# Inverting 64x64 triangular blocks of a recurrence: the lower levels in 32x32 tiles of TensorE on half the columns

## The reference

```python
def step(state, inp):
    r_t, w_t, k_t, v_t, kk_t, a_t = inp
    sa = jnp.einsum('bhvk,bhk->bhv', state, -kk_t)
    state = (state * w_t[:, :, None, :]
             + sa[..., None] * (kk_t * a_t)[:, :, None, :]
             + v_t[..., None] * k_t[:, :, None, :])
    return state, jnp.einsum('bhvk,bhk->bhv', state, r_t)
state0 = jnp.zeros((B, H, N, N), jnp.float32)
_, o = lax.scan(step, state0, ...)
```

## Time and profile before

| | |
|---|---|
| Median of 3 runs | 2298.42 us (2294.25 to 2299.28) |
| The profiled execution | 2297.4 us, its span 2295.6 us |
| Instructions in the span | 35212 |
| PE busy | 2162.0 us, 94% |
| DVE, ACT, POOL busy | 1228.8, 860.6, 996.5 us |
| The long stage of `rwkv` | from 210.5 us; levels 1 to 5 from 230.07 to 282.87; chunk loop from 297.1 |

### The profile page before, as it was taken

How to read it: one execution, slowest core, us unless ns; L and a number is a source line. 1 busy time by engine, 2 the same in 40 slices (tenths; PEclk the granted TensorE clock), 3 DMA queues, 4 the chain that set the end, 5 groups by cost and what they waited for, 6 DMA issues and landing times. The chain is left out here.

```text
span 2295.6 us, 35212 instructions
## 1 busy us (share of the span) xinstructions
PE 2162.0 (94%) x13161; PEld 1743.4 (76%) x13161; DVE 1228.8 (54%) x1928; ACT 860.6 (37%) x1345; POOL 996.5 (43%) x524
## 2 busy tenths in 40 slices
PE   6997998799999999899889999999999889999998
PEld 4675985688888888777667888888777568888887
DVE  3367526877505772432664577731398564777601
ACT  3445224433313332332364433332232754333322
POOL 4224111344534444365552444444456644444442
PEclk8999999899999999999899999999999999999999
DMA  4220012133332333233102333333333003333232
GB/s 126 65 65 25 4 30 61 56 102 99 110 91 84 100 91 110 78 83 83 46 1 60 88 101 101 91 90 97 102 75 91 1 19 92 95 101 97 87 101 87
DMA packets 347085, 177.10 MB, mean 77 GB/s; under 512 B 20835, under 2 KB 344158, under 8 KB 346974
## 3 DMA queue, kind: packets, MB, share of 16 engines
q1 hardware_dynamic: 346476, 175.47, 26.8%
q10 hardware_dynamic: 210, 0.08, 0.0%
q0 software_dynamic: 288, 0.03, 0.0%
HBM read 173.44 MB, written 2.11 MB: 76 GB/s over the span
## 5 line engine op out<-in xcount | busy, mean ns | idle before, releaser
L312 POOL TENSOR_TENSOR wlo<-raw,whi 128x1024 fp32r<-128x1024 f32 (+3 forms) x347 | 793.2, 2288 | 1081.6 <-ACT whi L871 603.8
L325 PE MATMUL banks<-xhi,whi 128*128 128x512 f32 x1688 | 668.8, 396 | 6.7 <-DVE cb L1034 3.9
L326 PE MATMUL banks<-xlo,whi 128*128 128x512 f32 x1688 | 659.0, 390 | 0.0
L327 PE MATMUL banks<-xhi,wlo 128*128 128x512 f32 x1688 | 658.9, 390 | 0.0
L325 PEld LDWEIGHTS banks<-xhi,whi 128*128 128x128 f32 x1688 | 318.1, 188 | 82.8 <-issue 13.6
L326 PEld LDWEIGHTS banks<-xlo,whi 128*128 128x128 f32 x1688 | 318.1, 188 | 68.2 <-issue 3.6
L327 PEld LDWEIGHTS banks<-xhi,wlo 128*128 128x128 f32 x1688 | 318.0, 188 | 67.0
L961 ACT ACTIVATE cb<-banks,conv 128x512 f32<-128x512 f32 x152 | 118.0, 779 | 438.7 <-DVE banks L1023 438.7
L871 ACT ACTIVATE whi<-raw 128x1024 fp32r<-128x1024 f32 (+2 forms) x208 | 204.9, 989 | 186.1 <-DMA raw<-in_ffn_w_out_dram 78.9
L326 PE MATMUL banks<-glo,whi 128*128 128x512 f32 x608 | 236.5, 389 | 0.0
L325 PE MATMUL banks<-ghi,whi 128*128 128x512 f32 x608 | 236.5, 389 | 0.0
(11 more groups left out here) (450 smaller groups left out, 2615.8 us busy)
## 6 DMA issues: line engine op xcount, KB each, us to landing
raw<-in_ffn_w_in_dram SPq DMA_DIRECT2D x88, 512.0 KB, 3.8
raw<-in_w_ffn_up_dram SPq DMA_DIRECT2D x64, 512.0 KB, 4.1
raw<-in_w_ffn_down_dram SPq DMA_DIRECT2D x32, 512.0 KB, 3.7
raw<-in_ev_w_in_dram SPq DMA_DIRECT2D x25, 512.0 KB, 4.0
raw<-in_ffn_w_out_dram SPq DMA_DIRECT2D x32, 384.0 KB, 3.4
raw<-in_ffn_w_out_dram SPq DMA_DIRECT2D x32, 320.0 KB, 3.3
raw<-in_od_w_in_dram SPq DMA_DIRECT2D x20, 512.0 KB, 3.9
raw<-in_w_in_dram SPq DMA_DIRECT2D x16, 512.0 KB, 3.8
```

Of the source, the lines that this page charges most:

```text
L312: return pool.tensor_tensor(wlo[c][:, 0:n, :], raw[b][:, 0:n, :], whi[c][:, 0:n, :].bitcast(F32), ALU.subtract)
L325: pe.matmul(acc, whi[b][:, k, :], hi(k), start=first and k == 0, stop=False)
L326: pe.matmul(acc, whi[b][:, k, :], lo(k), start=False, stop=False)
L327: mm = pe.matmul(acc, wlo[b][:, k, :], hi(k), start=False, stop=last and k == n - 1)
```

## The change

The levels up to blocks of 32 work on the two diagonal 32x32 blocks of each 64x64 matrix alone. T, the transposed seed `sTt` and pm keep 256 columns a tile: 8 heads of 32, where partition group g of 32 (of four) holds block g % 2 of chunk g // 2. A group of these kinds is 32 matmuls of 32x32, on the four diagonal tiles of the array in turn (`SPREAD`), into four banks of 64 columns, and a take-out has 128x256 values. There are two such bank sets, so a group waits for the group two before it (`held`). The level from 32 to 64 becomes two kinds: `plast` (16 matmuls into the lower group's partitions, copied by ACT) and `ttlast`, whose first matmuls (`up`) give the off-diagonal block and whose second transpose the lower diagonal block of T. A new kind `s0` transposes T for the seed (ACT), in place of POOL's eight operations; POOL now places the upper diagonal blocks in Tt, one operation a tile after `tt` of level 4. The turns stand ahead of `p0`. `nt`, `ak`, `y`, `w`, `u` and the chunk loop are as before. The packed masks have 9 parts of 64 columns in place of 10.

```diff
+                order = [("nt", t, 0) for t in range(NT)] + [("turn", x, 0) for x in range(8)]
+                FINE = len(order)
+                order += [(kind, t, 0) for kind in ("p0", "s0") for t in range(NT)]
+                for l in range(1, LEVELS - 1):
+                    for kind in ("p", "tt", "t"):
                         order += [(kind, t, l) for t in range(NT)]
+                order += [(kind, t, 0) for kind in ("plast", "ttlast") for t in range(NT)]
+                WIDE = len(order)
                 order += [(kind, t, 0) for kind in ("ak", "y", "w", "u") for t in range(NT)]
...
+                def held(n):
+
+                    if n < FINE or n >= WIDE + 4:
+                        return [n - 4] if n >= 4 else []
+                    if n < WIDE:
+                        return [n - 2] if n >= FINE + 2 else [n + (n - FINE) - 4, n + (n - FINE) - 3]
+                    return [WIDE - 2 + (n - WIDE) // 2]
...
+                SPREAD = [(g, (i + g) % 4, i // 4) for i in range(8) for g in range(4)]
...
+                def quad(n):
+                    return banks[:, 4 * (n % 2):4 * (n % 2) + 4, 0:2 * SUB].rearrange("p h (q n) -> p q h n", q=2)
...
                     for t in range(NT):
-                        wait_taken(pool, where["nt", t, 0])
-                        pool.tensor_tensor(four(Tt[:, t, :]), four(nt[:, t, :]), mask(TURNED), ALU.mult).then_inc(seeded.h, 1)
-                        pool.wait_ge(seeded.h, 2 * t + 1)
-                        pool.tensor_tensor(four(Tt[:, t, :]), four(Tt[:, t, :]), mask(EYE), ALU.add).then_inc(seeded.h, 1)
+                        wait_taken(pool, where["tt", t, LEVELS - 2])
+                        pool.tensor_scalar(Tt[:, t, :].rearrange("p (a s n) -> p a s n", a=8, s=2)[:, :, 0, :],
+                                           sTt[:, t, :].rearrange("p (a n) -> p a n", a=8), masks[:, WHERE, 0:1], None, ALU.mult)                            .then_inc(placed.h, 1)
...
+                        elif kind == "w":
+                            pe.wait_ge(placed.h, t + 1)
...
+                        elif FINE <= n < WIDE:
+                            for g, hh, q in SPREAD:
+                                x = sub(g)
+                                to = g + (1 if kind == "plast" else 0)
+                                if kind == "plast" and g % 2 or kind == "ttlast" and not g % 2:
+                                    continue
+                                o = banks[sub(to), 4 * (n % 2) + hh, q * SUB:(q + 1) * SUB]
+                                if kind == "p0":
+                                    mm = pe.matmul(o, nt[x, t, column(q, hh, g % 2)], ident[x, x], start=True, stop=True)
+                                elif kind == "s0":
+                                    mm = pe.matmul(o, T[x, t, small(q, hh)], ident[x, x], start=True, stop=True)
+                                elif kind == "t":
+                                    mm = pe.matmul(o, sTt[x, t, small(q, hh)], ident[x, x], start=True, stop=True)
+                                elif kind == "ttlast":
+                                    up = banks[sub(g - 1), 4 * (n % 2) + hh, q * SUB:(q + 1) * SUB]
+                                    pe.matmul(up, pm[x, t, small(q, hh)], sTt[x, t, small(q, hh)], start=True, stop=True)
+                                    mm = pe.matmul(o, T[x, t, small(q, hh)], ident[x, x], start=True, stop=True)
+                                elif kind in ("p", "plast"):
+                                    mm = pe.matmul(o, nt[x, t, column(q, hh, to % 2)], T[x, t, small(q, hh)], start=True, stop=True)
+                                else:
+                                    mm = pe.matmul(o, pm[x, t, small(q, hh)], sTt[x, t, small(q, hh)], start=True, stop=True)
...
                         elif kind == "p0":
-                            chain(dve.tensor_tensor(four(T[:, t, :]), acc, mask(0), ALU.mult))
-                            ins = dve.tensor_tensor(four(T[:, t, :]), four(T[:, t, :]), mask(EYE), ALU.add)
+                            chain(dve.tensor_tensor(smalls(T[:, t, :]), quad(n), small_mask(0), ALU.mult))
+                            ins = dve.tensor_tensor(smalls(T[:, t, :]), smalls(T[:, t, :]), small_mask(EYE), ALU.add)
...
+                        elif kind == "ttlast":
+                            ins = dve.tensor_copy(Tt[:, t, :].rearrange("p (q h s n) -> p q h s n", q=2, h=4, s=2)[:, :, :, 1, :], quad(n))
```

More of the change, by code:

```diff
@@ L32 @@
 EHALF = math.exp(-0.5)
-TURNED, BEFORE, UPTO, EYE = LEVELS, LEVELS + 1, LEVELS + 2, LEVELS + 3
+SUB = C // 2
+EYE, WHERE, BEFORE, UPTO = LEVELS - 1, LEVELS, LEVELS + 1, LEVELS + 2
 CST = {}
 _at = 0
-for _name, _w in (("ident", P), ("ones", P), ("pair", P), ("swap", P), ("packed", 10 * C), ("future", P), ("future_own", P),
+for _name, _w in (("ident", P), ("ones", P), ("pair", P), ("swap", P), ("packed", 9 * C), ("future", P), ("future_own", P),
                   ("inside", S), ("freq", 2), ("onehot", RLEN), ("flip", P)):
@@ L75, in constants @@
     ri, ci = row % C, col[:, 0:C]
-    levels = [(ri >> l + 1 == ci >> l + 1) & (ri >> l & 1 == 1) & (ci >> l & 1 == 0) for l in range(LEVELS)]
-    turned = (ri >> 1 == ci >> 1) & (ri & 1 == 0) & (ci & 1 == 1)
-    put("packed", np.concatenate(levels + [turned, ri < ci, ri <= ci, ri == ci], 1))
+    rs, cs = ri % SUB, ci % SUB
+    levels = [(rs >> l + 1 == cs >> l + 1) & (rs >> l & 1 == 1) & (cs >> l & 1 == 0) for l in range(LEVELS - 1)]
+    put("packed", np.concatenate(levels + [rs == cs, ri // SUB == ci // SUB, ri < ci, ri <= ci], 1))
     put("future", np.where(col > row, NEG, 0))
@@ L1250, in rwkv @@
             cs, ep, em, vt = (sb(ctx, n, [P, 4, S]) for n in ("cs", "ep", "em", "vt"))
-            masks = sb(ctx, "masks", [P, 10, C])
+            masks = sb(ctx, "masks", [P, 9, C])
             pc = sb(ctx, "pc", [P, 4, NCH])
@@ L1299, in rwkv @@
             with ExitStack() as c2:
-                T, Tt = f[:, 0:4, :], f[:, 4:8, :]
+                T, sTt = (f[:, i:i + 2, :].rearrange("p a (b w) -> p (a b) w", b=2) for i in (0, 2))
+                Tt = f[:, 4:8, :]
                 pm = sb(c2, "pm", [P, NT, S])
@@ L1305, in rwkv @@
                 s0 = state["s"]
-                made, took, copied, seeded, uppered, lowered = (
-                    sig(n) for n in ("made", "took", "copied", "seeded", "uppered", "lowered"))
+                made, took, copied, placed, uppered, lowered = (
+                    sig(n) for n in ("made", "took", "copied", "placed", "uppered", "lowered"))
                 read, u_done, kv_, z_done, produced, rtook, summed, otk, ftaken, decayed = (
                     sig(n) for n in ("read", "u_done", "kv", "z_done", "produced", "rtook", "summed", "otk", "ftaken", "decayed"))
[L1311 to L1314, removed]
+                order = [("nt", t, 0) for t in range(NT)] + [("turn", x, 0) for x in range(8)]
[3 more added lines that the diff above has]
+                    for kind in ("p", "tt", "t"):
                         order += [(kind, t, l) for t in range(NT)]
+                order += [(kind, t, 0) for kind in ("plast", "ttlast") for t in range(NT)]
+                WIDE = len(order)
                 order += [(kind, t, 0) for kind in ("ak", "y", "w", "u") for t in range(NT)]
                 where = {x: n for n, x in enumerate(order)}
-                BY_ACT = ("turn", "t", "y", "w", "u")
+                BY_ACT = ("turn", "s0", "t", "plast", "y", "w", "u")
                 nth = [sum((x[0] in BY_ACT) == (kind in BY_ACT) for x in order[:n]) for n, (kind, *_) in enumerate(order)]
@@ L1375, in _ @@
                     for n, (kind, t, l) in enumerate(order):
-                        if n >= 4:
-                            wait_taken(pe, n - 4)
+                        for x in held(n):
+                            wait_taken(pe, x)
                         if kind == "p0":
                             wait_taken(pe, where["nt", t, 0])
+                        elif kind == "s0":
+                            wait_taken(pe, where["p0", t, 0])
                         elif kind == "p":
@@ L1385, in _ @@
                             if l == 1:
-                                pe.wait_ge(seeded.h, 2 * t + 2)
+                                wait_taken(pe, where["s0", t, 0])
                         elif kind == "t":
                             wait_taken(pe, where["tt", t, l])
+                        elif kind == "plast":
+                            wait_taken(pe, where["t", t, LEVELS - 2])
+                        elif kind == "ttlast":
+                            wait_taken(pe, where["plast", t, 0])
+                        elif kind == "w":
+                            pe.wait_ge(placed.h, t + 1)
                         elif kind == "y":
@@ L1410, in _ @@
                                 o = two[q][part(c), hh * C:(hh + 1) * C]
[L1411 to L1419, removed]
+                                if kind == "y":
```

(5 more changed lines are left out.)

15 lines of the change are left out of this document (13 added, 2 removed).

## The result

The changed kernel takes **2354.83 us** (median of 4 runs, 2353.4 to 2358.56) against 2298.16 (4 runs, 2294.25 to 2299.28) of the kernel before: 1.0246 times as long, with a 95% interval of 1.0234 to 1.0258. The forecast was 2354, from 2340 to 2367. The profiled execution took 2353.4 us with a span of 2351.6, 56.0 more than before.

The account below looks back on a forecast made before the run. PE's instructions were taken to arrive in blocks of 256, about 3.65 us each. From 225.8 us, 34.8 blocks took 127.0 us, ending u at 352.8 instead of 297.1: +55.7 us on 2298.4, 2354 us, range 2340 to 2367.

Parts of the forecast that it names:

- Step 1: Matmuls of the inversion: 1024 more, giving 2048 more records with their weight loads, 4096 instructions or 16 blocks.
- Step 2: PE in the inversion: 7.3 to 29.1 ns a record, so a 256-instruction block takes 3.62 to 3.73 us, taken as 3.65.
- Step 3: Two bank sets instead of four: 0.43 us per 256-wide take-out, two groups about 1.25 us, hidden under the 3.65 us block.
- Step 4: Turns ahead of p0: fine work of the inversion starts at 225.8 us and not at 230.07.
- Step 5: POOL: eight seeding operations go, four placements of at most 1.28 us come; they and the later alo differences cost nothing.
- Step 6: ACT and DVE: extra s0 and plast copies and half-width operations stay hidden under the block time; smaller masks cost nothing.
- Step 7: ak, y, w, u unchanged at 14.2 us for four blocks; the first two groups' wait, below 1 us, fits inside a block.
- A: Rival for the inversion: instruction fetch hidden, eviction chain bounds, -19.7 us to 2279 us; chance 0.08.
- B: Rival for the inversion: fetch hidden, matmuls no faster than crossing ones at 20.2 ns, +20.9 us to 2319 us; chance 0.04.
- C: Rival for the inversion: clock falls and array corners do not overlap either, 48 us more, 2402 us; chance 0.04.

Follow-up runs that it names:

- e1: Kernel before with matmuls of p0, p, tt and t cut to 32 of 64 weight and 32 of 64 moving columns, same instruction count: 2298.40 us.
- e2: Changed kernel with half the matmuls in each 32x32 group, each with 64 moving columns in place of 32: 2299.45 us.
- e3: Kernel before with one small matmul ahead of every matmul of p0, p, tt and t, 3840 more PE instructions: 2348.38 us.
- e6: Kernel before with 32 small matmuls in each of the eight chunks of the chunk loop, 1024 more PE instructions: 2306.51 us.
- e4: Kernel before with only the eight turn groups moved ahead of p0: 2297.94 us.
- e5: Kernel before with turns first, plain 128x128 transposes for t and the seed, and p crossing corners, so fewer PE instructions: 2288.76 us.

## Why the prediction was right

*What bounds the kernel.* The point from which everything followed, that the stage stood at one block of 256 instructions per 3.62 us, rested on few rows: three pauses and a count. e1, e2 and e3 bear it out. Less work with the same count changed nothing, the changed kernel with half the count lost its whole loss, and the count alone, at the full clock, cost 49.1 us in the kernel before. The Trainium skill ("Runtime: NRT & Kernel Launch", Instruction fetch mechanics) has the fetch hidden. The traces here disagree wherever PE would get through a block in less than some 3.6 us; where it is slower, as in e6, they agree.

*Step 1, the count.* Right: 2048 more records and 16 more packets. The page has 4104 more instructions where 4096 were counted.

*Step 2, PE's rate.* The estimate was 7.3 ns a record. At the full clock the trace has one run of 128 records, in 1.35 us (at 224.18, below; the clock of 223.1 to 225.6 was 1.00): without the 0.24 of its last record 8.7 ns each, a little more than estimated. At the lower clock the burst of 127 takes 1.93 us, 13.3 ns each. As said ahead, it did not matter: the burst is half of a block.

*Step 2, the block.* 3.65 us taken. From p0's second group at 224.18 to the end of u at 352.61 the window below holds just the 4416 records counted. These 128.4 us are 3.69 for each of the 34.8 blocks. The term was a little too small, by 1.4 us in all.

```profile
224.20:352.60 128.40, 76.05 (x4416) 71.18 (x4416) 20.39 (x46) 15.77 (x35) 8.54 (x8) 0.56 0.02 5
```

*Step 3, two bank sets.* Take-outs of 256 columns last 0.42 us on DVE and 0.38 on ACT, for 0.43. DVE's and ACT's first of them, and PE between:

```profile
223.13 0.42 DVE L1555 TENSOR_TENSOR f<-banks,masks 128x256 f32<-128x256 f32 x1 [9.37 <-PE banks L1460]
...
224.18 1.35 PE L1460 MATMUL banks<-cst,oT 32*32 32x32 f32 x128 [1.09 <-ACT v L1594]
...
227.42 0.90 PE L1460 MATMUL banks<-cst,oT 32*32 32x32 f32 x49 [1.20 <-issue]
...
229.26 0.38 ACT L1597 ACTIVATE f<-banks 128x256 f32<-128x256 f32 x1 [5.19 <-PE banks L1462]
```

PE waited for them only at 225.90 (0.37 us), and 14 records later it stood for 1.20 us for its next block anyway.

*Step 4, the start.* 225.8 predicted, 224.18 found (the row above, released by the turn of v as foreseen). The step was right. Of the 1.6 us 1.5 come from ahead of the stage: its first matmul ran at 209.05 instead of 210.53, and other executions differ there as well (208.17 in e4, 207.16 in e5).

*Step 5, POOL.* Right, with room: the placements take 0.9 us each and the four alo behind them 4.92, done at 323.8. w starts at 344.7.

```profile
313.09 1.83 POOL L1395 TENSOR_SCALAR f<-f,masks 128x256 f32<-128x256 f32 x2 [94.72 <-DVE f L1560]
317.06 1.82 POOL L1395 TENSOR_SCALAR f<-f,masks 128x256 f32<-128x256 f32 x2 [2.14 <-DVE f L1560]
318.85 4.92 POOL L1399 TENSOR_TENSOR alo<-oT,ahi 128x512 fp32r<-128x512 f32 x4
```

*Step 6.* Right: from 230 to 330 us PE waited for neither ACT nor DVE.

*Step 7, ak to u.* 16.5 us by the windows, which leave out the last 0.5, not 14.2. The clock was 0.88 on average, and the longest pause was 1.11 us for the 0.61 of the earlier trace rows. Since the blocks already count these records, it stands in the 3.69 and isn't added.

```profile
349.89 2.72 PE L1479 MATMUL banks<-oT,f 64*64 64x64 f32 x85 [1.11 <-issue]
```

*The sum.* u ends at 349.89 + 2.72 = 352.61, where 352.8 was forecast; in the kernel before it ended at 297.30 (294.70 + 2.60), 0.2 behind the 297.1 that the sum took. So the stage gave +55.3, and 0.7 us is lost behind it, which was put at nothing and has no cause that was looked for. -1.6 of the start, +1.4 of the blocks, -0.2 of the base and +0.7 behind turn the 55.7 into 56.0, the difference of the spans. Two errors of over 1 us cancelled, so the hit within 1 us is luck, and the hit within 3 us is not.

*The rivals.* A needed blocks in under 1.3 us and B in 2.6 (two groups of 1.29): the shortest of the 29 steps was 3.42. C was half right, which the forecast gave a chance of 0.04 as a whole. The clock did fall, and for the whole inversion. Only its second condition, that the quarters of the array don't overlap, did not hold: a group of 64 records takes 64 x 13.3 = 0.85 us, not 2.6, even at 1.2 GHz. A forecast with the low clock as its expected case would have had the same time.

## What to carry to other kernels

Count instructions as well as columns. A float32 matmul of this program is four on PE's queue, and in this stage the queue was refilled by 256 instructions per 3.6 to 3.7 us on average, however idle the array was. So divide a stage's instructions by 256, multiply by 3.65, and compare with its span before making its blocks smaller. A PE that is busy for 99% may stand at both limits at once, and pauses called "issue" at equal counts of records are how the second one shows. The way out is fewer and larger operations (transposes of whole tiles in e5). More instructions are cheap only where a stage has room, as in e6.

## What the runs showed of the hardware

- The granted clock was 0.50 from 227.4 us to the end of the changed inversion, 0.51 on average over its 111.4 us, with PE busy for 60.7 of them. The low clock cost nothing there that can be seen, since each burst ended well before the next block. In e1 and e2, with PE busy for 24.75 and 27.26 of 40 us, it was 0.91 on average. In nt it was visible: the same kind got through 81 records in 2.60 us at 0.50, where it got through 129 at 1.00.
- Four 32x32 tiles of the array side by side gave a record in 13.3 ns at the lower clock and in 8.7 ns at the full one. The fastest before was 20.2 ns at the full one, for 64x64 corners that cross.
- Changing which half of rows goes with which half of columns, so that a group uses four corners of the array instead of two, moved 128 records of equal shape from 3.73 us to 2.5 (p in e5). Which property of the corners makes the difference was not measured.
- PE had no more than one packet ahead. In the changed kernel q8 brought one between 215 and 216 us and the next between 225 and 226, though PE waited for POOL's and ACT's work in between. By the count of 256 that second one came when PE had just entered a new block, 16 records into the run at 224.18, and PE ran out at 226.22 and went on only at 227.42. In the 36 us of the row of slices above no two packets stand closer than three slices. What inside the fetch takes the 3.6 us was not measured.
